# Delta rule's triangular inverse: the backward direction's blocks on the crossed tiles of TensorE's array

## The reference, cut to what matters

```
a_mat = jnp.where(strict, jnp.einsum("bhncd,bhnsd->bhncs", k_beta, k) * decay, 0.0)
t_mat = lax.linalg.triangular_solve(
    eye + a_mat, jnp.broadcast_to(eye, a_mat.shape),
    left_side=True, lower=True, unit_diagonal=True)
u = jnp.einsum("bhncs,bhnsv->bhncv", t_mat, v * beta[..., None])
...
o_fwd = gated_delta_chunked(qp, kp, vp, ...)
o_bwd = flip(gated_delta_chunked(flip(qp), flip(kp), flip(vp), ...))
```

## Time and profile before

| what | us |
|---|---|
| median of 3 runs | 3851.12 |
| lowest, highest of the runs | 3843.83, 3856.26 |
| span of the profiled execution, first to last instruction | 3845.8 |
| startup window of the delta stage (`invert(0)` beside `prepare(1)`) | 57.25 |
| windows of heads 0 to 6, first U of a head to the next | 80.7, 82.1, 82.5, 82.4, 84.0, 82.7, 69.8 |
| window of head 7 | 62.5 |

### The profile page before, as it was taken

How to read it: one execution, slowest core, us unless ns; L and a number is a source line. 1 busy time by engine, 2 the same in 40 slices (tenths; PEclk the granted TensorE clock), 3 DMA queues, 4 the chain that set the end, 5 groups by cost and what they waited for, 6 DMA issues and landing times. The chain is left out here.

```text
span 3845.8 us, 80099 instructions
## 1 busy us (share of the span) xinstructions
PE 3333.8 (87%) x33244; PEld 2800.3 (73%) x33244; DVE 1607.4 (42%) x2550; ACT 1015.1 (26%) x2016; POOL 478.1 (12%) x439
## 2 busy tenths in 40 slices
PE   8999998888879979999996699999968994987873
PEld 6877777788757759998996588888858873544431
DVE  3155753334336541115896345555434424111113
ACT  2122311122232120012553244455422110211112
POOL 1000000000000010001231222233111000222222
PEclk9999999999989979999997799999979996999997
DMA  4336465221245243234453301111006237999997
GB/s 126 98 116 206 156 207 174 88 53 44 88 176 179 90 112 95 88 92 139 161 189 111 103 24 40 51 44 36 25 20 228 73 96 280 418 419 418 413 414 299
DMA packets 314847, 595.22 MB, mean 155 GB/s; under 512 B 56993, under 2 KB 221706, under 8 KB 285590
## 3 DMA queue, kind: packets, MB, share of 16 engines
q1 hardware_dynamic: 263348, 455.68, 33.5%
q10 hardware_dynamic: 40329, 118.90, 8.7%
q0 software_dynamic: 10928, 17.08, 1.2%
HBM read 472.36 MB, written 139.97 MB: 159 GB/s over the span
## 5 line engine op out<-in xcount | busy, mean ns | idle before, releaser
L3240 PE MATMUL ex_bank_ps<-ex_w_gate_up_sb,ex_xT_sb 128*64 128x256 f32 x2240 | 281.2, 406 | 85.2 <-DMA ex_w_gate_up_sb<-in_w_up_e 79.6
L3240 PEld LDWEIGHTS ex_bank_ps<-ex_w_gate_up_sb,ex_xT_sb 128*64 128x64 f32 x2240 | 166.2, 140 | 212.3 <-issue 120.2
L260 DVE CAST in_w_hi_sb<-in_w_sb 128x1024 fp32r<-128x1024 f32 x119 | 81.9, 689 | 549.3 <-PE in2n_bank_ps L272 268.5
L272 PE MATMUL in2n_bank_ps<-in_h_hi_sb,in_w_hi_sb 128*128 128x352 f32 (+3 forms) x696 | 224.9, 323 | 2.1 <-DVE in_h_lo_sb L401 2.1
L272 PE MATMUL in2n_bank_ps<-in_h_lo_sb,in_w_hi_sb 128*128 128x352 f32 (+3 forms) x696 | 224.4, 322 | 0.0
L272 PE MATMUL in2n_bank_ps<-in_h_hi_sb,in_w_lo_sb 128*128 128x352 f32 (+3 forms) x696 | 223.9, 322 | 0.0
L1474 PE MATMUL mix_bank_ps<-mix_y_hi_sb,mix_wb_hi_sb 128*128 128x512 f32 (+2 forms) x480 | 170.6, 355 | 56.8 <-DVE mix_y_lo_sb L1705 44.0
L3431 DVE TENSOR_TENSOR ex_hidden_sb<-ex_silu_g_sb,ex_bank_ps 128x128 f32<-128x128 f32 x70 | 20.1, 287 | 440.1 <-ACT ex_silu_g_sb L3292 431.5
L272 PE MATMUL qkv_tile_bank_ps<-in_h_hi_sb,in_w_hi_sb 128*128 128x352 f32 (+1 forms) x576 | 186.2, 323 | 8.5 <-DVE qkv_ones_r_sb L1867 7.9
L272 PE MATMUL qkv_tile_bank_ps<-in_h_lo_sb,in_w_hi_sb 128*128 128x352 f32 (+1 forms) x576 | 185.5, 322 | 0.0
L272 PE MATMUL qkv_tile_bank_ps<-in_h_hi_sb,in_w_lo_sb 128*128 128x352 f32 (+1 forms) x576 | 185.2, 322 | 0.0
(11 more groups left out here) (474 smaller groups left out, 8252.6 us busy)
## 6 DMA issues: line engine op xcount, KB each, us to landing
ex_w_gate_up_sb<-in_w_gate_e SPq DMA_DIRECT2D x70, 1024.0 KB
ex_w_gate_up_sb<-in_w_up_e SPq DMA_DIRECT2D x70, 1024.0 KB
ex_w_down_sb<-in_w_down_e SPq DMA_DIRECT2D x70, 1024.0 KB
in_w_sb<-in_w_in SPq DMA_DIRECT2D x118, 512.0 KB
scr_pT<-in_o_sb ACTq DMA_DIRECT2D x65, 512.0 KB
scr_p2T<-in_o_sb ACTq DMA_DIRECT2D x52, 520.0 KB
qkv_x_sb<-scr_p2T SPq DMA_DIRECT2D x8, 1560.0 KB, 8.5
mix_gate_sb<-scr_pT SPq DMA_DIRECT2D x24, 512.0 KB
```

The costliest lines, as they stand in the source:

```text
L260: dve.tensor_copy(self.w_hi[:, s, :, 0:width], w).then_inc(self.w_hi_rdy, 1)
L272: last = pe.matmul(self.psum(s, n)[:width, 0:m], w_[:, s, k, 0:width], h_[:, k, a:a + m], start=(k == 0 and z == 0), stop=(k == KT - 1 and ...
L3240: last = t.matmul(bank[m * BT:(m + 1) * BT, GU_B + b % 2, 0:2 * P], xT[:, s, k, at:at + BT], wgu[:, ws, :, k, m::M], start=(k == 0), stop= ...
```

## The change

The units change from 5 units of 4 matrices to NU = 3 units of 4, 3 and 3 chunks, each with both directions. The forward direction stays on the diagonal tiles ("straight"). The backward direction is "crossed": the matmul reads one half of the partitions and writes the other, which is the tile off the diagonal. In each round N and NT change partitions together. P stays where it is because its product is made from NT+1: (NT+1)·P lands as the whole new P. For that, GpSimd adds 1 to the crossed NT of each unit (`nti`, new buffer `nt_and_one`, L2969), and VectorE copies the crossed product instead of adding it.

```diff
-        U_B, DS_B, O_B, NT_B, P_B, A_B = 0, 1, 2, 3, 5, 7
+        U_B, DS_B, O_B, NT_B, P_B, A_B = 0, 1, 2, (3, 4), (5, 6), 7
...
-        NU = 2 * NCH // 4
-        mats = lambda u: range(4 * u, 4 * u + 4)
+        NU = 3
+        unit_at = (0, 4, 7, NCH)
...
-        weight = {"n": 5, "NT": 10, "P": 5, "pt": 6, "ym": 6, "w": 6}
+        weight = {"n": 6, "NT": 9, "P": 5, "pt": 6, "ym": 6, "w": 6}
...
+                def crossed(b, at, lhsT, rhs):
+                    for p in part:
+                        last = t.matmul(bank[other(p), b, at * CA:(at + 1) * CA], lhsT(p), rhs(p), start=True, stop=True)
+                    return last
...
                 def product(i):
...
                     ab.wait(t, h, "NT", r, u)
+                    gx.wait(t, h, "nti", r, u)
+
+                    if i:
+                        vb.wait(t, h, "P", *powers[i - 1])
+                        vx.wait(t, h, "P", *powers[i - 1])
...
-                    if i >= 2:
-                        vb.wait_all(t, h, *(("P", *powers[j]) for j in (i - 2, i - NU) if j >= 0))
-                    b = p_bank(("P", r, u))
-                    for j, m in enumerate(mats(u)):
-                        for p in part:
-                            last = t.matmul(bank[p, b, j * CA:(j + 1) * CA], nt(r, m, p), pc[p, m, :], start=True, stop=True)
+                    for j, c in enumerate(unit(u)):
+                        last = straight(P_B[0], j, lambda p: nt(r, 0, c, p), lambda p: pc[p, c, :])
+                        last_x = crossed(P_B[1], j, lambda p: nti[p, c, :], lambda p: pc[p, NCH + c, :])
...
                     else:
-                        ab.wait(t, h, "NT", *powers[i - 2])
+                        ab.wait(t, h, "NT", *powers[i - 1])
+                        ax.wait(t, h, "NT", *powers[i - 1])
...
VectorE:
-                    vb.step(v.tensor_tensor(pc[:, m, :], pc[:, m, :], blocks(p_bank(("P", r, u)), 4), ALU.add), "P", r, u)
+                    vb.step(v.tensor_tensor(pc[:, us(u), :], pc[:, us(u), :], blocks(P_B[0], k), ALU.add), "P", r, u)
+                    px.wait(v, h, "P", r, u)
+                    vx.step(v.tensor_copy(pc[:, us(u, 1), :], blocks(P_B[1], k)), "P", r, u)
...
ScalarE:
+                    for d, pe, act in ((0, pb, ab), (1, px, ax)):
+                        pe.wait(a_, h, "NT", r, u)
+                        if r < ROUNDS:
+                            ins = a_.activation(nn[:, r % 2, us(u, d), :, :].rearrange("p m x w -> p (m x w)"), bank[:, NT_B[d], 0:2 * k * CA], ACT.Copy)
...
GpSimd:
-                for f in range(NF):
+                for f in (0, 2):
...
+                for r, u in powers:
+                    yield b_place["NT", r, u]
+                    ax.wait(g_, h, "NT", r, u)
+                    gx.step(g_.tensor_tensor(nti[:, us(u), :], nn[:, r % 2, us(u, 1), 1, :],
+                                             eye[:, :].unsqueeze(1).broadcast_to([P, len(unit(u)), CA]), ALU.add), "nti", r, u)
```

More of the change, by code:

```diff
@@ L2522, in prepare @@
                     pa.step(last, x, g)
-                for u in range(NU):
+                for u in range(TU):
                     yield a_place["T", u]
@@ L2535, in invert, with straight @@
                 s = h % 2
-                nt = lambda r, m, p: nt0[p, s, m // NCH, m % NCH, p] if r == 0 else nn[p, r % 2, m, 1, :]
-                n = lambda r, m, p: nn[p, r % 2, m, 0, :]
+                nt = lambda r, d, c, p: nt0[p, s, d, c, p] if r == 0 else nn[p, r % 2, d * NCH + c, 1, :]
+                n = lambda r, d, c, p: nn[p, r % 2, d * NCH + c, 0, :]
+                other = lambda p: part[1 - part.index(p)]
+                def straight(b, at, lhsT, rhs):
+                    for p in part:
+                        last = t.matmul(bank[p, b, at * CA:(at + 1) * CA], lhsT(p), rhs(p), start=True, stop=True)
+                    return last
+                def crossed(b, at, lhsT, rhs):
+                    for p in part:
+                        last = t.matmul(bank[other(p), b, at * CA:(at + 1) * CA], lhsT(p), rhs(p), start=True, stop=True)
+                    return last
+                eye_of = lambda p: ident[p, p]
                 for f in range(NF):
@@ L2545, in invert @@
                         ab.wait(t, h, "n", 0)
-                    b = nt_bank(("n", f))
-                    for j, m in enumerate(fill(f)):
-                        for p in part:
-                            last = t.matmul(bank[p, b, j * CA:(j + 1) * CA], nt(0, m, p), ident[p, p], start=True, stop=True)
+                    for j in range(len(fill[f])):
+                        d, c = fill[f][j]
+                        last = straight(fill_bank[f], j, lambda p: nt(0, d, c, p), eye_of)
+                        if f < 2 and j < len(cross[f]):
+                            last_x = crossed((NT_B[1], P_B[1])[f], j, lambda p: nt(0, 1, cross[f][j], p), eye_of)
                     pb.step(last, "n", f)
+                    if f < 2:
+                        px.step(last_x, "n", f)
                 def product(i):
@@ L2574, in invert @@
+                    for j, c in enumerate(unit(u)):
                         if r < ROUNDS:
-                            for p in part:
-                                t.matmul(bank[p, b, 2 * j * CA:(2 * j + 1) * CA], nt(r - 1, m, p), n(r - 1, m, p), start=True, stop=True)
-                        at = (2 * j + 1 if r < ROUNDS else j) * CA
-                        for p in part:
-                            last = t.matmul(bank[p, b, at:at + CA], n(r - 1, m, p), nt(r - 1, m, p), start=True, stop=True)
+                            straight(NT_B[0], 2 * j, lambda p: nt(r - 1, 0, c, p), lambda p: n(r - 1, 0, c, p))
+                            crossed(NT_B[1], 2 * j, lambda p: nt(r - 1, 1, c, p), lambda p: n(r - 1, 1, c, p))
+                        at = 2 * j + 1 if r < ROUNDS else j
+                        last = straight(NT_B[0], at, lambda p: n(r - 1, 0, c, p), lambda p: nt(r - 1, 0, c, p))
+                        last_x = crossed(NT_B[1], at, lambda p: n(r - 1, 1, c, p), lambda p: nt(r - 1, 1, c, p))
@@ L2592, in invert @@
                             p = part[d]
-                            last = t.matmul(bank[p, b, j * CA:(j + 1) * CA], pc[p, d * NCH + c, :], ident[p, p], start=True, stop=True)
+                            last = t.matmul(bank[p, NT_B[g], j * CA:(j + 1) * CA], pc[p, d * NCH + c, :], ident[p, p], start=True, stop=True)
                     pb.step(last, "pt", g)
@@ L2600, in invert @@
                             to, of = part[d], part[1 - d]
[L2601 to L2602 removed]
+                            last = t.matmul(bank[to, P_B[g], j * CA:(j + 1) * CA], nt0[of, s, d, c, to], pc[of, d * NCH + c, :], start=True, stop=True)
+                    px.step(last, "ym", g)
                 for g in halves:
@@ L2888, in _ @@
         def _(g_):
-            for plan in (ga, gb, gd):
+            for plan in (ga, gb, gx, gd):
                 plan.begin(g_)
```

121 lines of the change are left out of this document (67 added, 54 removed).

## The result

The changed kernel runs in 3798.49 us (median of 4 runs, 3797.91 to 3802.43) against 3850.34 us before (median of 4, 3843.83 to 3856.26): the ratio is 0.9865, with a 95% interval of 0.985 to 0.9879. It is faster by 51.9 us, where the forecast said 43 (3808 us, with a range of its own of 3795 to 3822). The profiled executions differ by 49.2 us in span (3796.6 and 3845.8).

What follows compares the result with a forecast made beforehand. TensorE was taken as the middle windows' bound, with GpSimd's order deciding ahead of place 8. Heads 1 to 5 -22.5, startup -4.9, head 0 -5.4, head 6 -10.5: -43.3 from 3851.1 gives 3808 us; own range 3795 to 3822, for all 3768 to 3862.

Steps and rivals of the forecast that it cites:

- The rate: TensorE's NT and P records: 14.6 ns each with four tiles at work, freeing 16.4 us per window with an inverse.
- rival 1: TensorE's feeding sets the rate: 29.2 ns a record, nothing saved, waits remain; +35 us, 3886; chance 0.12.
- The first part of a middle window: From fill n to the P unit of place 8: GpSimd's chain decides, 28.5 us in place of 25.8.
- rival 3: GpSimd's chain does not bind ahead of place 8: 6.5 us more in six windows, about -86 us, 3765; chance 0.13.
- The part behind place 8: From the P unit of place 8 to the next fill: TensorE stays the bound, 49.5 us in place of 56.6.
- 10.2 in place of 11.2, +1.8 for the recurrence's floor, +1.3 for single banks: Behind place 8: 10.2 us saved as units' ends share nothing; 1.8 given back to recurrence, 1.3 to waits for copies.
- Heads 0 and 6: Windows of heads 0 and 6: 80.7 to 75.3 us (-5.4) and 69.8 to 59.3 us (-10.5).
- Startup: Startup window: second triangle, `nti`, unit cycles and closing work give 52.4 us in place of 57.25, -4.9.
- eleven unit cycles of about 2.15: Startup window, after the second triangle and `nti`: eleven further unit cycles take 23.7 us.
- Head 7: 0: Head 7's window has no inverse, so the change leaves its time alone: 0 us.
- Rival 4: TensorE's clock falls to 0.5 for 10 us in each of six windows: gives back 5 us each, 3838; chance 0.17.
- the granted clock stays at 1.00 in them: Sign to look for: TensorE's clock stays full in the windows; a fall inside them would make the prediction wrong.

Runs made afterwards that it cites:

- experiment 2: Changed kernel with both directions on the diagonal tiles and without GpSimd's `nti`; larger units and single banks stay: 3874.3 us, ratio 1.0056 to the kernel before.
- experiment 4: Changed kernel without GpSimd's NT+1, the crossed P computed as NT times P (output not the reference's): 3794.5 us, ratio 0.9845 to the kernel before.
- experiment 8: Changed kernel without GpSimd's NT+1, plus spare matmuls: 14 in each window of heads 0 to 5, two ahead of each last-head U and dS: 3774.3 us.
- experiment 7: Changed kernel with two spare matmuls ahead of each U and dS of the last head, and 14 in each window of heads 0 to 5: 3776.6 us.
- experiment 6: Changed kernel with four spare matmuls ahead of each U and dS in the last head's recurrence: 3784.5 us, ratio 0.9823 to the kernel before.
- experiment 5: Changed kernel with two spare matmuls ahead of each U and dS in the last head's recurrence: 3790.6 us, ratio 0.9838 to the kernel before.

## Why the prediction was right, and where it was wrong

**The rate: right.** 14.6 ns was forecast from five rows, and 15 ns measured over units of 48 and 64. The opposite bound, 29.2, is what experiment 2 has, and it ended on the other side of no change, as rival 1 said (3874 measured without `nti`, 3886 in the rival). The 25 ns of the Trainium skill's page "TensorE: Matmul & The Clock Gate", Part 1 ("Wait — 56ns, not 53.3ns?"), do not hold across tiles: records on different tiles start 6 to 7 ns apart here. What does hold is 58 ns from one record to the next on the same tile.

**The first part of a middle window: the number right, the reason half of it, and luck in both.** 28.5 was forecast, 28.4 measured at nearly full clock, and the row above shows P waiting for GpSimd. Inside the number two errors cancel: the chain began 12.0 us after the fill (2490.17), not 11.0, and took 15.6 us to the end of the last triangle, not 16.9, since the power took 1.96 us instead of 2.94. And the forecast took GpSimd for the only thing in the way. Its rival 3 (-86 us if the chain did not bind) was an error: experiments 4 and 8 took `nti` out and came to 1 to 8 us in all, and to 0.8 us in the one pair of middle windows with full clock on both sides. ScalarE's queue (squares, copies for the transposes, table load, exponentials) ends only about that much sooner. The forecast had added up ScalarE's part only as far as the start of GpSimd's chain. Experiment 2 says the same from another side: with no `nti` at all, and TensorE at the old rate, this part was 28.5 us too.

**The part behind place 8: the terms given back were not there.** The step "10.2 in place of 11.2, +1.8 for the recurrence's floor, +1.3 for single banks" made 49.5 us. Measured were 45.87, which is 10.8 less than 56.64. Of the 11.2 us only 0.4 were lost, where the three terms gave back 4.1. Experiment 2 measured the larger units and the single banks together, at the old rate: 56.48, no cost. Which of the terms was the most wrong, no run tells apart. This mis-sized step is worth 3.6 us in each of five windows, 18 us. The clock took some of it back: over heads 1 to 5 the part behind place 8 was 46.3 us on average, and the first part 29.3 in place of 28.5. And 2.8 us more came from the kernel before: heads 1 and 5 had 83.67 and 84.27 us there, and the forecast reckoned all five by the middle window.

**Heads 0 and 6: near.** -6.7 and -11.8 were measured, -5.4 and -10.5 forecast. The forecast took their windows before from the first U, 80.7 and 69.8, but its terms from the fill, from where they are 79.1 and 72.25. In head 0 place 8 came at 27.2 us, not at 25.8, and the part behind it took 45.3 us, not 49.5.

**Startup: wrong.** -4.9 was forecast, +1.1 measured. P of place 8 came 23.2 us after the fill, as reckoned (23.0); the other 35.1 us had been put at 29.4. The step "eleven unit cycles of about 2.15" left out the work of prepare that stands between the units on TensorE (its matmuls take 8.4 us there), and 7 us of this part ran at half clock. `nti` has a share too: without it the window was 4.6 us (experiment 4) and 3.8 us (experiment 8) shorter.

**Head 7 and the clock: the rival that came true in part.** The step "Head 7: 0" failed by 5.3 us. Rival 4 said that the clock could fall in stretches of each window and take the gain to 3838. It did fall, in windows 0 to 5 and at startup, and took a quarter to a half of the 30 us that the rival had given it: experiment 7 puts its price at 8 us against experiment 6 and at 14 against experiment 5. Single executions wander by as much: the windows of heads 0 to 5 add up to 450.7, 448.3 and 444.6 us in the changed kernel and in experiments 5 and 6, which have the same code there, and to 441.1 in experiment 7. The forecast's own claim, "the granted clock stays at 1.00 in them", was wrong, and it had named a fall of the clock as a sign of being wrong.

**The total.** By windows the result is 5.7 us beyond the forecast: heads 1 to 5 by 14.5, heads 0 and 6 by 2.6, less 6.0 at startup and 5.3 in head 7. The medians differ by 3 us more, which is within what runs of one kernel differ. So the main mechanism was right, four tiles at twice the rate and no gain ahead of place 8, and the total came this close by luck: errors of both signs, 14.5 us in heads 1 to 5 against 11.3 at startup and in head 7.
